# Latent attention: a turn's sum of probabilities issued behind the next turn's maxima

## What is computed

```python
def _mla_attention(q_nope, q_rope, k_nope, k_rope, v):
    scale = (Dn + Dr) ** -0.5                       # 64 + 32 rows, 16 heads
    def blk(args):                                  # one block of 128 queries
        b, qnb, qrb = args
        t = b * Q_BLOCK + jnp.arange(Q_BLOCK)
        s = (jnp.einsum('bqhd,bkhd->bhqk', qnb, k_nope)
             + jnp.einsum('bqhd,bkd->bhqk', qrb, k_rope)).astype(jnp.float32) * scale
        pr = jax.nn.softmax(jnp.where(kpos[None, :] <= t[:, None], s, NEG_INF), axis=-1)
        return jnp.einsum('bhqk,bkhd->bqhd', pr.astype(v.dtype), v)
```

## Time and profile before

| | us |
|---|---|
| median of 3 runs | 3054.64 (3053.04 to 3061.67) |
| the profiled execution, device time | 3053.61 |
| its span, first to last instruction | 3051.8 |
| latent attention within it | about 1685 to 2624 |
| DVE, busy share of the span | 64% |
| PE, busy share of the span | 95% |

### The profile page before, as it was taken

How to read it: one execution, slowest core, us unless ns; L and a number is a source line. 1 busy time by engine, 2 the same in 40 slices (tenths; PEclk the granted TensorE clock), 3 DMA queues, 4 the chain that set the end, 5 groups by cost and what they waited for, 6 DMA issues and landing times. The chain is left out here.

```text
span 3051.8 us, 41224 instructions
## 1 busy us (share of the span) xinstructions
PE 2892.7 (95%) x13411; PEld 2328.4 (76%) x13411; DVE 1938.8 (64%) x3398; ACT 1590.5 (52%) x2808; POOL 1392.0 (46%) x1139
## 2 busy tenths in 40 slices
PE   8999996888999999999998799999999999899998
PEld 6888884566888788777877588888888878688776
DVE  4543315663578864555664588888888887357875
ACT  3111114666445544444544277777777777534643
POOL 0022104665232540001440388888888889423353
PEclk9999997999999999999999699999999999999999
DMA  5343437565997675455799634435335342498674
GB/s 165 84 136 125 117 118 242 179 203 172 308 277 239 201 247 183 159 177 167 251 328 380 148 73 102 103 73 116 91 78 127 73 92 87 157 301 270 212 243 145
DMA packets 284760, 530.13 MB, mean 174 GB/s; under 512 B 29200, under 2 KB 110992, under 8 KB 277392
## 3 DMA queue, kind: packets, MB, share of 16 engines
q1 hardware_dynamic: 218528, 391.22, 43.3%
q10 hardware_dynamic: 66032, 136.48, 14.7%
HBM read 346.85 MB, written 180.49 MB: 173 GB/s over the span
## 5 line engine op out<-in xcount | busy, mean ns | idle before, releaser
L2609 POOL TENSOR_TENSOR mla_pl<-mla_p,mla_ph 128x512 fp32r<-128x512 f32 (+3 forms) x640 | 702.9, 1121 | 144.4 <-ACT mla_p L2458 141.5
L1523 PE MATMUL end_bank<-end_xh,end_whi 128*128 128x512 f32 x1808 | 718.1, 397 | 44.3 <-DVE end_wlo L1754 17.0
L1525 PE MATMUL end_bank<-end_xh,end_wlo 128*128 128x512 f32 x1808 | 708.2, 392 | 0.0
L1524 PE MATMUL end_bank<-end_xl,end_whi 128*128 128x512 f32 x1808 | 707.6, 391 | 0.0
L1592 ACT CAST end_whi<-early_wraw 128x1024 fp32r<-128x1024 f32 (+1 forms) x204 | 211.4, 1036 | 531.8 <-PE end_bank L1525 510.7
L2457 ACT ACTIVATE mla_ph<-mla_score 128x512 fp32r<-128x512 f32 (+3 forms) x640 | 342.4, 535 | 238.0 <-PE mla_score L2285 232.9
L1754 DVE TENSOR_TENSOR end_wlo<-early_wraw,end_whi 128x1024 fp32r<-128x1024 f32 x188 | 255.4, 1358 | 317.9 <-ACT end_whi L1592 317.7
L1523 PEld LDWEIGHTS end_bank<-end_xh,end_whi 128*128 128x128 f32 x1808 | 342.1, 189 | 134.9 <-DVE end_wlo L1754 24.6
L2542 DVE TENSOR_TENSOR mla_acc<-mla_acc,mla_p 128x512 f32<-128x512 f32 (+3 forms) x576 | 351.0, 609 | 106.6 <-ACT mla_p L2458 104.2
L1524 PEld LDWEIGHTS end_bank<-end_xl,end_whi 128*128 128x128 f32 x1808 | 342.3, 189 | 72.6 <-issue 2.9
L1525 PEld LDWEIGHTS end_bank<-end_xh,end_wlo 128*128 128x128 f32 x1808 | 341.6, 189 | 72.4
(11 more groups left out here) (242 smaller groups left out, 4985.7 us busy)
## 6 DMA issues: line engine op xcount, KB each, us to landing
early_wraw<-in_pe_gate ACTq DMA_DIRECT2D x64, 512.0 KB, 4.9
early_wraw<-in_w_out ACTq DMA_DIRECT2D x62, 512.0 KB, 7.3
early_wraw<-in_w_in ACTq DMA_DIRECT2D x56, 512.0 KB, 3.8
scratch_q<-in_rope SPq DMA_DIRECT2D x64, 256.0 KB, 2.9
swa_q<-scratch_q SPq DMA_DIRECT2D x8, 2048.0 KB, 9.2
end_factor<-scratch_inv SPq DMA_DIRECT2D x64, 256.0 KB, 9.6
scratch_proj<-end_out_f SPq DMA_DIRECT2D x64, 256.0 KB, 6.9
scratch_sum<-end_out_f SPq DMA_DIRECT2D x64, 256.0 KB, 6.3
```

Of the source, the lines that this page charges most:

```text
L1523: nc.tensor.matmul(bank, wh[:, at], xh[:, k0 + k * nq, :], start=(k == 0), stop=False)
L1524: nc.tensor.matmul(bank, wh[:, at], xl[:, k0 + k * nq, :], start=False, stop=False)
L1525: last = nc.tensor.matmul(bank, wl[:, at], xh[:, k0 + k * nq, :], start=False, stop=(k == kc - 1))
L2609: pool.tensor_tensor(p_lo[b][:, off:TC], prob[b][:, off:TC], p_hi[b][:, off:TC].bitcast(F32), ALU.subtract).then_inc(p_lo_ok, 1)
```

## The change

DVE's order within a turn is altered. In turn g it now issues `add(g - 1)` behind the items of turn g, not `add(g)`. So that a chunk's sum is still complete at the end of the chunk, the last turn of a chunk issues both `add(g - 1)` and `add(g)`, one behind the other. In the first turn of a chunk there is nothing to add. No instruction, wait or buffer is added or removed.

```diff
                     for v, n in at_slot(u, k):
                         item(v, n)
-                    add(g)
+                    if not st["first"]:
+                        add(g - 1)
+                    if st["last"]:
+                        add(g)
                     for e in turns_at(u, k, 0):
                         gather(e)
```

## The result

The changed kernel takes 3077.36 us (median of 4, 3071.61 to 3080.96) against 3053.86 us (3053.04 to 3061.67) on the same chip: a ratio of 1.0069 with an interval of 1.0047 to 1.0092. It is slower, as forecast, but by 23.5 us where 13 were forecast, and it lies above the range.

The account below looks back on a forecast made before the run. PE's instruction stream was taken as the bound: 0.43 + 0.31 + 0.31 - 0.11 = +0.94 us a head, +13.2 over fourteen heads, -0.4 in the first, +12.8 on 3053.6; 3067 us stated for a median, range 3055 to 3072.

Parts of the forecast that it names:

- turn 0: Start of a head: the add ahead still waits for the last probabilities, PE's largest wait is untouched; counted 0.
- first item of turn 4, on DVE: End of chunk 0: DVE starts this item at 2014.54 instead of 2013.99, behind the moved add.
- PE, by turn 6: End of chunk 0: PE's item of turn 5 under way at 2015.04 instead of 2014.61; loss 0.43 us.
- PE, turn 13: End of chunk 1: PE's second item under way at 2026.88 instead of 2026.57, behind two dependent adds; loss 0.31 us.
- PE, turn 22: Ordinary turns: turn 21's maxima start 0.11 us earlier, so PE's 0.30 us loss here shrinks by 0.11.
- PE, turn 25: End of chunk 2: PE's second item under way at 2044.07 instead of 2043.76, behind two dependent adds; loss 0.31 us.
- a head: Sum of one head's losses and gain, +0.94 us, in fourteen heads, the second to the fifteenth: +13.2.
- the first one: The opening reading of the latent attention's steady part: PE busy 113.5 of 115 us, granted clock 1.00.
- The first head: PE gains 0.87 us at the gather, waits at turns 19 and 23 shrink 0.3, chunk 2's end loses 0.8; net about -0.4.
- The maxima freed: Rival: chunk-end maxima still come in time, so only gains remain, 0.30 us at turn 22 per head; 3049 us, chance 0.13.
- The dependent add costs no more: Rival: each of three chunk ends loses 0.19 us less, a head +0.37, the whole +4.6; 3059 us, chance 0.20.
- ACT late: Rival: ACT's third exponential waits for the last sum at two chunk starts per head, 0.3 us a head; 3071 us, chance 0.12.

Follow-up runs that it names:

- e3: The kernel before with one more DVE instruction (384 columns, result unread) ahead of the first item of turn 4, second to fifteenth head: 3065.09 us, ratio 1.0025.
- e2: The kernel before with the new order of adds in chunk 0 of every head only: 3062.79 us, ratio 1.0019; again, one execution, 3068.44 us.
- e4: The changed kernel with PE's wait at turn 5 filled by two matmuls of 512 columns whose result is overwritten: 3072.77 us, ratio 1.0045.
- e1: The changed kernel with chunk 0 of every head back in the old order of adds, chunks 1 to 3 in the new: 3065.34 us, ratio 1.0022.
- e5: The changed kernel with a chunk's last two adds parted, the earlier ahead of the last turn's items: 3063.05 us, ratio 1.0019.
- e12: The changed kernel with one more DVE instruction (384 columns) ahead of the first item of turn 4, second to fifteenth head: 3104.83 us, ratio 1.0153.
- e7: The changed kernel with ACT's copy of a chunk's denominators ahead of the exponentials of its turn: 3064.94 us, ratio 1.0027.
- e10: e5 with e7's early copy and a head's last add moved behind the first two items of the next head: 3057.25 us, ratio 0.9993.
- e11: The kernel before with e7's early copy, a head's last add behind the next head's first two items, the first head's gather before its add: 3050.48 us, ratio 0.9965.

## Why the prediction was wrong in size

**The place and the size of the waits held.** All times in the table are from the start of a head (2006.37 before, 2009.42 after).

| step | predicted | measured |
|---|---|---|
| turn 0 | 0 | 0 |
| first item of turn 4, on DVE | +0.55 | +0.52 (7.62 to 8.14) |
| PE, by turn 6 | +0.43 | +0.41 |
| PE, turn 13 | +0.31 | +0.28 |
| PE, turn 22 | -0.11 | -0.10 |
| PE, turn 25 | +0.31 | +0.29 |
| a head | +0.94 | +0.83 |

DVE's timeline of the changed kernel at turns 3 and 4 answers to the earlier trace rows:

```profile
2015.17 0.69 DVE L2486 TENSOR_REDUCE mla_mx<-mla_mx 128x1 f32<-128x512 f32 x1 [0.82 <-PE mla_mx L2285]
2015.78 0.42 DVE L2542 TENSOR_TENSOR mla_acc<-mla_acc,mla_p 128x256 f32<-128x256 f32 x1
2016.29 0.56 DVE L2541 COPY mla_acc<-mla_acc 128x384 f32<-128x384 f32 x1
2016.76 0.28 DVE L2542 TENSOR_TENSOR mla_acc<-mla_acc,mla_p 128x128 f32<-128x128 f32 x1
2016.96 0.67 DVE L2556 TENSOR_TENSOR mla_o_sum<-mla_o,mla_o_low 64x512 f32<-64x512 f32 x1
2017.56 0.28 DVE L2490 CUSTOM_DVE_ANT_0 mla_mx<-mla_mx,const_causal_q 128x128 f32<-128x128 f32 x1
```

The reader should see that DVE now idles 0.82 us ahead of the maximum, where the add used to be done, and that six instructions then stand in a row. The idle time was cover, and the change left it empty. On PE, the item of turn 5 and its neighbours:

```profile
2017.39 0.42 PE L2285 MATMUL mla_score<-mla_q,mla_k 96*128 96x384 f32 x1
2017.95 0.39 PE L2285 MATMUL mla_mx<-early_k,early_q 96*128 96x256 f32 x1
2018.18 0.28 PE L2285 MATMUL mla_o<-mla_ph,mla_v 128*128 128x256 f32 x1
```

The item is recorded 8.53 us into the head where the earlier trace rows has 8.24, and the next matmul follows after 0.23 where 256 columns take 0.12: 0.29 and 0.11, together 0.40, which is the loss. It shows as a start that is later and a record that is longer, with no wait put beside it; I had expected a wait in the row. The list of waits hides it too: PE's two rows of waits for a maximum grew only from 14 and 9 entries to 16 and 10.

Turns 11 to 13 and 25, against the earlier trace rows: two adds together on DVE, and PE's two items in 0.84 and 0.79 us where both pairs took 0.51.

```profile
2028.04 1.51 DVE L2542 TENSOR_TENSOR mla_acc<-mla_acc,mla_p 128x512 f32<-128x512 f32 x2
...
2029.75 0.84 PE L2285 MATMUL mla_mx<-early_k,early_q 96*128 96x512 f32 x2
...
2047.26 0.79 PE L2285 MATMUL mla_mx<-early_k,early_q 96*128 96x256 f32 x2
```

The 0.05 that the rows of the table leave over is lost again at turns 33 to 37. Fourteen heads at 0.83 make 11.6 where 13.2 were counted. So far the sum was 1.6 too high.

**The step that failed is the first one:** The earlier trace rows was read as saying that the granted clock is 1.00 in this stage, and the sum took it as staying there. It priced every added wait of PE at its own length. No term of the sum and no rival had the clock in it. The row says only that the clock was 1.00 with the idle time that PE had then. With 0.41 us more of it at turn 5, the clock fell in 6 of 14 heads in the first trace and in 5 of 14 in the second, and that cost 13.8 and, at 5 times 1.57, 7.9 us. With this term the sum would have been 12.8 + 8 to 14, or 3074 to 3081, around the measured time.

That the falls come from PE's idle time around turn 5 is shown by several runs together. They are there with the old order of adds and a late item (e3, one fall) and with the new order in chunk 0 alone (e2 again). They are absent with the new order where the wait is filled (e4) or not made (e1, e5), and more frequent when it is longer (e12). Counted over all traces, in the second to the fifteenth head: 0 in 28 heads of the kernel before; 11 in 28 of the changed one; 4 in 42 with the loss at turn 5 alone (e2 twice, e3); 0 in 42 without an added idle PE there (e1, e4, e5); 0 in 14 with turn 7's idle time taken away (e7); 0 in 28 of e10 and e11, which have neither; 8 in 14 with a longer wait at turn 5 (e12).

The single traces are few for a rate. If heads fell independently, a rate of four in ten would be absent from fourteen by chance in about one case of 1,300 (0.6 to the 14th), and one in ten (the rate of e2 and e3) in one case of four, but from the 42 of e1, e4 and e5 in one of 80. Since e2 had none in one execution and three in the other, heads of one execution may not be independent. Counted by executions instead, five of the six with the unfilled wait and turn 7's idle time show falls in these heads, and none of the eight others; by chance that would come out so in one case of about 330. e4 and e7 each rest on one trace.

What stays open is why one head falls and its neighbour with the same timeline does not, and why e2 and e3 fall less often than the changed kernel, although PE's turns 3 to 7 look alike. The changed kernel also loses time at turns 13 and 25, 30 us and more ahead of the next head's turn 7; with turn 5 left alone (e1) these losses set off nothing.

**The first head** gained 1.4 and not 0.4, and here too the clock had been left out of the sum. The turned maxima came 0.82 earlier (1733.02 against the earlier trace rows's 1733.84; 0.87 was counted):

```profile
1733.02 0.28 PE L2308 MATMUL mla_mx<-const_ident,mla_m_all 128*8 128x128 f32 x1
```

Windows of what follows, of the kernel before and of the changed one. The clock had just risen to 1.00 in both:

```profile
1736.00:1738.00 2.00, 1.87 (x8) 1.48 (x7) 1.51 (x7) 1.14 (x3) 1.50 (x2) 0.50 0.01 2
1738.00:1740.00 2.00, 2.00 (x6) 1.57 (x5) 1.08 (x2) 0.99 (x2) 0.49 (x1) 0.50 0.00 0
1740.00:1742.00 2.00, 2.00 (x7) 1.23 (x6) 1.34 (x4) 0.09 (x1) 1.28 (x1) 0.50 0.47 131
```

```profile
1736.00:1738.00 2.00, 2.00 (x12) 1.66 (x10) 1.88 (x6) 1.27 (x4) 1.53 (x2) 1.00 0.01 2
1738.00:1740.00 2.00, 1.12 (x6) 0.51 (x4) 1.90 (x5) 1.21 (x3) 1.33 (x2) 1.00 0.49 130
1740.00:1742.00 2.00, 1.71 (x9) 1.43 (x10) 1.20 (x5) 0.76 (x2) 1.22 (x1) 1.00 0.02 5
```

Before, PE had stood idle for 0.71 us at turn 9 and lost its clock again 2 us behind it; after, it had not stood idle there and kept it. From 1732.5 before and 1732.0 after to the end of the head, the mean clock is 0.93 of 50.29 us and 0.99 of 48.90, which is 7.0 against 1.0 us at half clock. At 1.57 in 3.4 these 6 us are worth 2.8. With the 0.87 that makes 3.7, of which 1.4 is left: the rest would have gone into longer waits of PE behind pairs of adds (its idle 1.17 us at 1739.1 to 1740.3, in the second and third row, is the largest, and the item there waits for a maximum behind two adds). I had counted 0.8 for these. No run was made for this sum, so it is argued and not shown. The clock's part in it is borne out by the other traces. All nine with the `gather` ahead of the add at turn 8 have no fall that begins behind turn 9, and their first head takes 80.2 to 81.5 us. Of the five with the old order there, four have one, of 3.4 to 10.2 us, that begins 1.9 to 4.1 us behind turn 9's product; in the fifth, the kernel before again, the clock was at half already. These five take 81.4 to 85.0 us.

**The rivals.** "The maxima freed" failed by its own condition: the maxima at the chunk ends did not come in time. At turn 22 it said that the whole 0.30 us would go, and 0.10 of it did; the first head gained 1.4 where it said 1.2, in part by the clock. "The dependent add costs no more" is refuted: two adds of 512 columns in succession take 1.51 and 1.47 us, two independent maxima of 0.69 take 1.28. The rule of the Trainium skill ("VectorE: DVE Perf Modes", "The DRAIN you can't avoid") that a semaphore between DVE operations costs nothing extra, measured there on eight copies, does not hold for this pair. "ACT late" is refuted: ACT's third exponential waited for the sum once from 1700 to 2560 us, for 0.2 us. A wait of 1.2 us of its first exponential, put down to DVE's add, stands there once too, but such waits (1.0 and 1.2) are also in the kernel before again.

## What to carry to other kernels

An idle spell of an engine ahead of its urgent work is cover: an operation that waits there costs nothing, and moved behind the urgent work it lengthens the busy stretch that the other engine waits for. A wait's total (79 us here, halved by the change) says nothing of its worth; ask who is late at its end. And where PE is nearly full, price an added idle spell of PE twice: its own length, and the clock; look for other short idle spells nearby. Here, in the traces of e4 and e7, it was enough to fill or remove one of the two.

## What the runs showed of the hardware

- With 0.41 us more of idle time at turn 5, the granted clock could fall from 2.4 to 1.2 GHz some 3 us later, in the changed kernel ten times for 3.4 us and once for 13.7. A short fall cost 1.57 us, almost four times the idle time that set it off.
- A single pause may do it too. In the last head two matmuls start 0.61 us apart in the kernel before, as they wait for ACT's copy, and in four of eleven traces with that wait the clock fell for 3.4 us right behind it; in three without the wait it did not.
- In the first head it went the other way: with the idle spell of 0.71 us at turn 9 removed, the clock stayed up to the end of the head, once it had risen, in nine traces of nine. With it, in four of five, the clock fell again.
- The same program with the same timeline loses it in some heads and not in others, and in other heads in the next execution.
- A DVE add that depends on the one ahead starts 0.09 to 0.10 us behind its end, at 512 columns as at 128; an independent instruction starts 0.09 before it.
